# A weight double sum formed by accumulating transfers instead of on VectorE, and one more seven-product pair in each hidden layer's down projection

## What is computed

```python
def squared_relu_mlp(h, w_up, w_down):              # 2 layers: mlp0, mlp1; inner width 4096
    return jnp.square(jax.nn.relu(h @ w_up)) @ w_down

def swiglu(h, w_in, w_out):                         # 4 layers: ffn00, ffn01, ffn10, ffn11; inner width 2816
    gate, up = jnp.split(h @ w_in, 2, axis=-1)
    return (jax.nn.silu(gate) * up) @ w_out
x = x + 0.5 * swiglu(rms_norm_2(x, g), w_in, w_out)
```

## Time and profile before

| | |
|---|---|
| median of three runs | 1616.55 us |
| profiled execution | 1616.26 us, span 1614.5 us |
| outside the span | 1.8 us |
| TensorE (PE) busy | 1600.7 us, 99% of the span, 9237 matmuls |
| VectorE busy | 1277.4 us, 79% |
| ScalarE busy | 964.4 us, 60% |
| transfers | 292.83 MB, mean 181 GB/s |

### The profile page before, as it was taken

The page is one execution under the profiler, slowest core; times in us unless marked ns, Lnnn a source line. Parts: engine busy times, 40 slices in busy tenths (PEclk is TensorE's granted clock), DMA queues, the critical chain, the costliest instruction groups (busy, mean ns, idle before and its releaser), DMA issues.

```text
span 1614.5 us, 25621 instructions
## 1 busy us (share of the span) xinstructions
PE 1600.7 (99%) x9237; PEld 1348.6 (84%) x9237; DVE 1277.4 (79%) x1884; ACT 964.4 (60%) x1466; POOL 88.6 (5%) x117
## 2 busy tenths in 40 slices
PE   9999999999999999999999999999999999999998
PEld 7888888887778888888888888888888888788886
DVE  5987898875969889788884757888878787778887
ACT  7743655555866555666554636665566655866654
POOL 1441000011000000100000000000010000100000
PEclk9999999999999999999999999999999999999999
DMA  8322554573125545555466445554655546245553
GB/s 333 137 101 106 208 182 187 212 289 131 53 81 207 182 182 209 195 199 190 180 244 245 179 157 182 184 195 172 231 186 186 202 182 218 96 154 185 191 193 111
DMA packets 41522, 292.83 MB, mean 181 GB/s; under 512 B 4928, under 2 KB 4960, under 8 KB 7008
## 3 DMA queue, kind: packets, MB, share of 16 engines
q1 hardware_dynamic: 40032, 283.05, 48.1%
q0 software_dynamic: 1264, 8.41, 1.5%
q10 hardware_dynamic: 144, 0.26, 0.0%
HBM read 290.65 MB, written 1.05 MB: 181 GB/s over the span
## 4 chain that ended last, share of the span: by engine, by line
PE 95%; ACT 2%; DVE 2%; issue 1%; POOL 0%; POOLq 0%; DVEq 0%; ACTq 0%
PE ps L785 27%; PE ps L791 14%; PE ps L749 11%; PE ps L751 11%; PE ps L760 11%; PE ps L846 3%; PE ps L850 3%; PE ps L847 3%; PE ps L871 1%; PE ps L1275 1%; PE ps L1077 1%; PE ps L1078 1%; PE ps L1086 1%; PE ps L1597 1%; PE ps L1583 1%
## 5 line engine op out<-in xcount | busy, mean ns | idle before, releaser
L2485 DVE TENSOR_TENSOR w_lo<-raw,w_hi 128x1024 fp32r<-128x1024 f32 x460 | 547.5, 1215 | 102.8 <-ACT w_hi L1769 102.2
L1769 ACT ACTIVATE w_hi<-raw 128x1024 fp32r<-128x1024 f32 x459 | 462.4, 1038 | 131.3 <-PE ps L760 111.8
L785 PE MATMUL ps<-h_both,w_hi 128*128 128x512 f32 x1920 | 461.5, 391 | 0.4 <-DVE h_both L2565 0.3
L785 PEld LDWEIGHTS ps<-h_both,w_hi 128*128 128x128 f32 x1920 | 352.1, 188 | 69.8 <-issue 1.7
L791 PEld LDWEIGHTS ps<-h_both,w_lo 128*128 128x128 f32 x1920 | 247.7, 191 | 10.4
L791 PE MATMUL ps<-h_both,w_lo 128*128 128x256 f32 x1920 | 250.9, 283 | 0.0
L1906 ACT ACTIVATE tm<-ps 128x512 f32<-128x512 f32 x120 | 71.7, 598 | 180.6 <-PE ps L791 180.3
L749 PE MATMUL ps<-w_hi,hid_hi 128*128 128x512 f32 x436 | 170.5, 391 | 0.0
L751 PE MATMUL ps<-w_hi,hid_lo 128*128 128x512 f32 x436 | 169.8, 389 | 0.0
L2642 DVE TENSOR_TENSOR tm<-ps,tm 128x512 f32<-128x512 f32 x120 | 82.9, 691 | 93.8 <-ACT tm L1906 93.3
L749 PE MATMUL ps<-w_hi,h_both 128*128 128x512 f32 x368 | 146.7, 399 | 0.5 <-DVE h_both L2565 0.5
(11 more groups left out here) (423 smaller groups left out, 1989.9 us busy)
## 6 DMA issues: line engine op xcount, KB each, us to landing
raw<-in_stream SPq DMA_DIRECT2D x264, 1024.0 KB, 4.8
ns_w<-in_ns_w POOLq DMA_DIRECT2D x1, 4096.0 KB, 17.4
ln_rows<-in_ln_rows POOLq DMA_DIRECT2D x2, 1024.0 KB, 10.2
row_const<-in_const_rest SPq DMA_DIRECT2D x1, 1076.0 KB, 19.3
raw<-in_second_halves SPq DMA_DIRECT2D x2, 512.0 KB, 6.8
x_sb<-in_x SPq DMA_DIRECT2D x1, 1024.0 KB, 9.1
row_const<-in_fin_rows POOLq DMA_DIRECT2D x2, 512.0 KB, 7.4
out<-x_row SPq DMA_DIRECT2D x3, 256.0 KB, 2.5
```

The costliest lines, as they stand in the source:

```text
L785: pe.matmul(bank[c], w_hi[:, slot, cols], h_both[:, :, k, :], start=(k == 0), stop=False)
L1769: act.activation(w_hi[:, static % 2, part], raw[:, r % RING, part], ACT.Copy).then_inc(hi_ready, 1)
L2485: dve.tensor_tensor(w_lo[:, static % 2, part], raw[:, r % RING, part], w_hi[:, static % 2, part].bitcast(F32), ALU.subtract).then_inc(lo_r ...
```

## The change

1. `seven_pairs`: seven pairs instead of six in the mlp layers, five instead of four in the ffn layers.
2. The order of panels becomes `OSOSSOSSOSSO` (mlp) and `OSOSSOSS` (ffn) for column half 0 and all S panels, then the tail. An ffn layer has three full O panels a half instead of three full and one of two blocks; an mlp layer four full and one of two blocks instead of five full.
3. The weight sums T1 and T3, which `w_sums` held, come from transfers: SyncE loads weight block 3 of the panel a second time into a buffer of 512 columns (`t3_even`, printed `t_even`, for even n; `mlp_t` or `ffn_t` for odd n), and GpSimd (POOL) issues two transfers that add block 0 to block 3 in `raw`, and block 2 to the second copy. For n from 2 on, the second copy is loaded when S(n-2) has been split, behind the panel load that waits for the same; `more` and the high part of sums half 0 wait for both adds (`t_summed`).
4. VectorE: the instruction of line 2500 goes; the low part of sums half 0 becomes two of 512 columns, as does its high part on ScalarE. The blocks stand in another order in the slots, and so do the operands of the four products.
5. In ffn layers x11 is folded behind the split of tail panel 1, and x21 behind that of tail panel 2; the transposes stand ahead of tail panel 2, as before (which now is the last). In ffn11 the last two panels that run tile by tile are full ones.
6. Some semaphores are shared to free numbers for the new ones; `junk` shares its place with `t3_even`.

```diff
 def seven_pairs(kt):
     if kt == FF // P:
-        return [4 * n + 2 for n in range(6)]
-    return [4 * n + 2 for n in range(4)]
+        return [4 * n + 2 for n in range(7)]
+    return [4 * n + 2 for n in range(5)]
...
+            pattern = "OSOSSOSSOSSO" if kt == FF // P else "OSOSSOSS"
...
+            def load_third(layer, n):
+                q = prod[layer + "_down"]
+                if n == 0:
+                    sp.wait_ge(ss_ready, squares_until(layer))
+                elif n == 1:
+                    sp.wait_ge(s_lo_ready, sevens_before[layer] + len(q.pairs))
+                else:
+                    sp.wait_ge(lo_ready, 2 * q.place[("S", n - 2)] + 4)
+                r = q.raw + q.order.index(("S", n))
+                sp.dma_start(third_sums(layer, n)[:, :], dram["stream"][r - 2, :, 3 * NB:]).then_inc(t3_loaded[n % 2], 16)
...
+                    behind = q.order.index(("S", n)) + 1 if n < 2 else q.order.index(("S", n - 2)) + RING
...
@@ ScalarE split_seven
                     elif s == 2:
                         act.wait_ge(w_used, v)
-                        act.wait_ge(seven_step, steps_before(layer) + 3 * n + 1)
-                        dst, src = w_hi[:, (v + 1) % 2, 0:2 * NB], w_sums[:, :, :].rearrange("p s n -> p (s n)")
+                        act.wait_ge(t_summed[n % 2], 32 * thirds_until(layer, n))
+                        act.activation(w_hi[:, (v + 1) % 2, 2 * NB:3 * NB], raw[:, r % RING, 3 * NB:], ACT.Copy)
+                        dst, src = w_hi[:, (v + 1) % 2, 3 * NB:], third_sums(layer, n)[:, :]
                     else:
-                        act.wait_ge(seven_step, steps_before(layer) + 3 * n + 3)
-                        dst, src = w_hi[:, (v + 1) % 2, 2 * NB:4 * NB], raw[:, r % RING, 2 * NB:4 * NB]
+                        act.wait_ge(seven_step, steps_before(layer) + 2 * n + 2)
+                        dst, src = w_hi[:, (v + 1) % 2, 0:2 * NB], raw[:, r % RING, NB:3 * NB]
...
@@ VectorE split_seven
-                    if s == "sums":
...
-                        dve.tensor_tensor(w_sums[:, :, :], panel.rearrange("p (m n) -> p m n", n=NB)[:, 0:3:2, :],
-                                          b12.unsqueeze(1).broadcast_to([P, 2, NB]), ALU.add).then_inc(seven_step, 1)
...
+                    if s == "more":
+                        dve.wait_ge(t_summed[n % 2], 32 * thirds_until(layer, n))
+                        dve.wait_ge(lo_ready, 2 * v + 2)
+                        dve.tensor_tensor(b22, t1, b22, ALU.add).then_inc(seven_step, 1)
                         dve.wait_ge(seven_step, done + 1)
...
+                        dve.tensor_tensor(b21, b22, b21, ALU.add).then_inc(seven_step, 1)
+                        continue
+                    dve.wait_ge(hi_ready, 2 * v + s + 1)
+                    if s == 2:
+                        dve.tensor_tensor(w_lo[:, (v + 1) % 2, 2 * NB:3 * NB], t1,
+                                          w_hi[:, (v + 1) % 2, 2 * NB:3 * NB].bitcast(F32), ALU.subtract)
...
+            def add_sums(layer):
+                q = prod[layer + "_down"]
+                for n in range(len(q.pairs)):
+                    r = q.raw + q.order.index(("S", n))
+                    pool.wait_ge(t3_loaded[n % 2], 16 * thirds_until(layer, n))
+                    pool.wait_ge(raw_full[r % RING], 16 * (r // RING + 1))
+                    pool.dma_start(raw[:, r % RING, 3 * NB:], dram["stream"][r - 2, :, 0:NB],
+                                   accum_op=ALU.add).then_inc(t_summed[n % 2], 16)
+                    pool.dma_start(third_sums(layer, n)[:, :], dram["stream"][r - 2, :, 2 * NB:3 * NB],
+                                   accum_op=ALU.add).then_inc(t_summed[n % 2], 16)
```

More of the change, by code:

```diff
@@ L83, in __init__ @@
         if self.pairs:
[L84 to L90, removed]
+            pattern = "OSOSSOSSOSSO" if kt == FF // P else "OSOSSOSS"
+            count = {"O": 0, "S": 0}
+            for kind in pattern:
+                self.order += (("S", count["S"]),) if kind == "S" else (("O", 0, count["O"]),)
+                count[kind] += 1
+            self.order += tuple(("O", 1, j) for j in range(self.per))
             self.place, at = {}, panel
@@ L424, in build @@
         seven_step = sem("seven_step")
+        t3_loaded = [sem(f"t3_loaded{i}") for i in range(2)]
+        t_summed = [sem(f"t_summed{i}") for i in range(2)]
         hid_z = sem("hid_z")
@@ L607, in steps_before, with third_sums, thirds_until, squares_until @@
         def steps_before(layer):
-            return 3 * sevens_before[layer] + 9 * hidden_layers.index(layer)
+            return 2 * sevens_before[layer] + 9 * hidden_layers.index(layer)
+        def third_sums(layer, n):
+            if n % 2 == 0:
+                return t3_even
+            return mlp_t if layer[:3] == "mlp" else ffn_t
+        def thirds_until(layer, n):
+            before = [len(prod[a + "_down"].pairs) for a in hidden_layers[:hidden_layers.index(layer)]]
+            return sum((c + 1 - n % 2) // 2 for c in before) + n // 2 + 1
+        def squares_until(layer):
+            return sums_before(layer) + (3 * TT if after_final(layer) else TT)
         PROD_BANK = {"p1": 6, "p5": 7, "q6": 4, "p7": 5}
@@ L697, in _ @@
                     load(q % RING, q, raw_last[q - RING])
+                    for layer, n in thirds.get(q, ()):
+                        load_third(layer, n)
                     q += 1
@@ L950, in hidden_layer @@
                         pe.wait_ge(t_lo, t0 + down.ks[min(PK * (j + 1), down.kt) - 1] // f_count + 1)
-                    if b == 1 and j == down.per - 2 and early_norm(layer):
+                    if b == 1 and j == down.per - f_count and early_norm(layer):
                         norm_batch(early_norm(layer), 0)
@@ L2486, in split, with split_seven @@
                                       w_hi[:, static % 2, part].bitcast(F32), ALU.subtract).then_inc(lo_ready, 1)
-            def split_seven(layer, q, n, w_sums, parts=("sums", 0, 1, "more", 2, 3)):
+            def split_seven(layer, q, n, parts=(0, 1, "more", 2, 3)):
                 v = q.place[("S", n)]
@@ L2762, in hidden_layer @@
                             rows_out(0, 2, last_x)
-                        fold(layer, down, 1)
+                        fold(layer, down, "x2")
                         if early_norm(layer):
                             norm_store(early_norm(layer), 0)
-                    split(down, b, b, 0, j)
+                        if f_count == 2:
+                            split(down, b, b, 0, j)
                 pending.append((down, 1, rstd_out))
```

208 lines of the change are left out of this document (107 added, 101 removed).

## The result

The changed kernel takes **1687.65 us** (median of four runs, 1686.89 to 1694.46) against 1616.35 us (1616.12 to 1616.74) on the same chip: ratio 1.045, interval 1.0439 to 1.0464, 71 us slower. The forecast was 1628 us, in 1614 to 1640. The direction was right, the size was not.

What follows compares the result with a forecast made beforehand. TensorE was taken as the bound, busy 1600.7 of 1614.5 us. The terms -4.1 - 1.2 + 9.7 + 1.8 + 0.1 + 5.6 = +11.9 us on 1616.26 gave 1628 us, range 1614 to 1640.

Steps and rivals of the forecast that it cites:

- Fewer matmuls: One pair more in each of six layers: 18 matmuls fewer, -4.1 us; ffn stalls gone, -1.2 us.
- The stalls: ffn down projections, last S behind a short O panel: 0.30 us lost in each of four layers, to go: -1.2 us.
- S behind S: Adjacent S panels: VectorE/ScalarE chain of 8.29 us against 7.71 due; 0.69 us lost by each second S, 9.7 us.
- couples: Pairs of neighbouring S panels, three per mlp layer, two per ffn layer, 14 in all; 0.69 us lost in each.
- x21: Its fold behind tail panel 2 makes the transposes 0.60 us late in three ffn layers: 1.8 us.
- The end of ffn11: Last panels: a 1.5 us wait goes, but token tile 1 starts 1.6 us late; together about nothing, +0.1 us.
- The sum of these: All terms except late transfers: 1616.3 - 4.1 - 1.2 + 9.7 + 1.8 + 0.1 = 1622.6 us.
- The new transfers: Second copies and adds late by 0 to 1.0 us, taken as 0.7 at 8 events, S(3) and S(5): 5.6 us.
- the right loop: From release of S(n-2)'s buffer through second copy to both adds landed: 9.4 to 13.0 us, where 12.0 are free.
- the collision: Next panel load and second copy go out with the adds, putting 3.6 us ahead of them: 9.4 becomes 13.0 us.
- The half-rate rival: Adds move at half the rate, 1.4 us more per pair, lateness 2.1 at 8 events: 1639 us; chance 0.18.

Runs made afterwards that it cites:

- experiment 6: Changed kernel without adding transfers, plus idle ScalarE work ahead of the sums of S(2) in the four ffn layers: 1646.55 us, ratio 1.0191.
- experiment 7: Changed kernel with the second copy, from the third S panel of a layer on, issued ahead of the 1 MB panel load: 1678.09 us, ratio 1.0381.

## Why the prediction was right or wrong

- **Fewer matmuls** (-4.1 and -1.2): 9219 matmuls, as forecast. The -4.1 wasn't measured apart. The stalls lost 1.3 us before, by TensorE's starts, and aren't there in the new order.
- **S behind S** (9.7): confirmed, the mechanism and the size: 9.4 us in 14 couples without adds, by TensorE's starts. In the changed kernel S(3) of ffn00 started at 847.15 and the third product of S(4)'s sums turn at 855.37, 8.22 us later; forecast 8.29.
- **x21** (1.8): it waits in three layers, as forecast, but the transposes start late by less: in the changed kernel at 868.71, due at 867.30 + 4 x 0.227 = 868.21, 0.50 us, so about 1.5 in all.
- **The end of ffn11** (0.1): from the last matmul of an S panel to the end of the span it was 27.5 us before, with 12 matmuls more (2.7 us), and 24.9 without adds: 0.1 more, as forecast.
- **The sum of these** is 1622.6 against 1622.24 measured without adds, and the terms agree one by one, so this part isn't luck.
- **The new transfers** (5.6): the step that failed. The forecast built the right loop with the right free time (12.0 us) and the wrong length: 13.0 at most, where it is 17.4. The second copy was to land 5.9 us behind the release, and GpSimd, which waits for it, started at 8.3 (825.76 less 817.46). Most of this is the panel load ahead of it: it landed 7.1 us behind its issue and not 4.8, with S(1)'s adds (issued at 814.47 and 815.02, the second one 7.1 us to its landing) still under way and the next panel load sent at 819.76. The later add was to land 2.9 us behind its issue, or 6.5 with the next load ahead of it, and took 8.6. The 2.9 came from one row of a 192 KB copy; here two adds at twice the engine time of a copy run beside another panel load and another copy. Each piece was priced by the row of one transfer, and the collision was added once, for one of them. The late panels were also others: S(2) and S(6), not S(3) and S(5). From S(2) on all S panels have the same loop, three panels long. That the first one that waits gives the next one time is a reading of the timelines, not shown by a run.
- **What no term held:** the half clock behind the long waits, 18.6 us. With delays of 0 to 1.0 the rows gave no reason for it. Nor did a term hold the 2.0 us at the end of the program.
- **The half-rate rival** (1639) had the right size for a part of it: the factor is about 2. But its price, 1.4 us more for a pair, is the engine time alone; it kept the loop of 13.0.

Counted from the starts of TensorE's matmuls less 0.227 for each, the S panels of the changed kernel lose 71.6 us: 18.6 by the clock and 53.0 in waits, of which the couples alone would be 9.4. So the 70.6 us of span are -5.3 for matmuls and the old stalls, about 1.5 for x21, 53.0 for waits, 18.6 for the clock, 0.1 for the end of ffn11 and 2.0 for the end of the program: 69.9. The remaining 0.7 isn't assigned.

## What to carry to other kernels

Price a transfer on a loop by when it can start and when it must have landed, with everything that shares the engines in that stretch, not by its own bytes: here the same adds cost 65 us or 2, by an issue one or two panels earlier into two more buffers. A buffer more changes nothing while the place on the issuing queue stays. And before an engine's instruction is turned into transfers, try the kernel with the transfers left out: that run (1622.2 us) said that nothing could be won here.

## What the hardware showed that I had not expected

- An adding transfer took 1.64 us of the 16 engines for 256 KB, a copy of the same bytes on the same queue 0.80. GpSimd was held 0.86 us by the first of a pair and 1.20 by the second. At the end of the program GpSimd's closing instruction took 6.56 us instead of 2.07, and the span ended 2.0 later.
- Behind waits of 4.1 us and more TensorE ran its next 8 to 14 matmuls 0.427 us apart instead of 0.227, with the granted clock at about half. In the kernel of experiment 6 a wait of 4.69 us so cost 1.7 to 2.3 us more. The same happened behind one wait of 2.8 us (ffn11), and in experiment 7 behind one of 1.6 us; the waits of 1.2 and 1.5 us in ffn01 and ffn10 of the changed kernel weren't followed by it.
